# Narrow products of the mixing layers in three one-pass matmuls behind the first tile, FOX's log-sigmoid in ACT's second slot, values turned in the middle of a tile

## The reference

```python
for i in range(DEPTH):                       # first block, DEPTH = 4
    y = rmsnorm(h, norm_mix[i])
    mix = mixer(y, w_in[i], ...)             # FOX, GLA, GDN, FOX
    h = h + mix
    h = h + swiglu(rmsnorm(h, norm_ffn[i]), w_gate_up[i], w_down[i])
# FOX: y @ w_in = q, k, v, gate (1024 columns each) and f (16 columns)
#      q, k get a norm over each head; the scores get the running sum of log_sigmoid(f + b_f)
# GLA: y @ w_in = q, k (512 each), v, gate (1024 each) and a_lr (16 columns)
#      alpha = log_sigmoid(a_lr @ w_alpha2 + b_alpha) / 16
# GDN: y @ w_in = q, k, v, gate (1024 each), a (8 columns) and beta (8 columns)
#      g = -exp(a_log) * softplus(a + dt_bias), beta = sigmoid(beta)
```

## Time and profile before

| | |
|---|---|
| median of three runs | 2555.58 us |
| profiled execution, its span | 2551.63 us, 2549.8 us |
| TensorE matmul (PE) | 2338.9 us busy, 92% |
| TensorE weight load (PEld) | 2195.9 us, 86% |
| VectorE (DVE) | 1566.3 us, 61% |
| ScalarE (ACT) | 1215.1 us, 48% |
| GpSimd (POOL) | 621.2 us, 24% |
| DMA | 342.94 MB, mean 134 GB/s |
| TensorE clock granted, mean | 0.962 of full speed |
| ACT table loads | 71, of 1.28 us |

### The profile page before, as it was taken

The page is one execution under the profiler, slowest core; times in us unless marked ns, Lnnn a source line. Parts: engine busy times, 40 slices in busy tenths (PEclk is TensorE's granted clock), DMA queues, the critical chain, the costliest instruction groups (busy, mean ns, idle before and its releaser), DMA issues. The chain is left out here.

```text
span 2549.8 us, 47516 instructions
## 1 busy us (share of the span) xinstructions
PE 2338.9 (92%) x19162; PEld 2195.9 (86%) x19162; DVE 1566.3 (61%) x2510; ACT 1215.1 (48%) x1859; POOL 621.2 (24%) x744
## 2 busy tenths in 40 slices
PE   4999999899999898799989899996898998889998
PEld 3888999798998687699977789995698998778998
DVE  4665654645654665465546656546667975656994
ACT  4455544444543642455345554443445554444653
POOL 3114211013211030032121132213174540053550
PEclk8889999999999999899999999998999999989999
DMA  4223545323555221155442245453243554233554
GB/s 160 84 83 133 180 154 189 123 83 122 176 162 169 100 68 51 51 168 179 155 144 84 90 136 173 160 189 121 83 163 120 189 165 166 67 119 130 189 171 136
DMA packets 52715, 342.94 MB, mean 134 GB/s; under 512 B 5888, under 2 KB 7104, under 8 KB 20160
## 3 DMA queue, kind: packets, MB, share of 16 engines
q1 hardware_dynamic: 51984, 336.26, 39.9%
q0 software_dynamic: 560, 4.26, 0.4%
HBM read 339.38 MB, written 1.05 MB: 134 GB/s over the span
## 5 line engine op out<-in xcount | busy, mean ns | idle before, releaser
L729 PE MATMUL ps<-arena_r,ring_hi 128*128 128x272 f32 (+1 forms) x6688 | 1605.5, 289 | 15.6 <-DVE arena L2107 7.4
L729 PEld LDWEIGHTS ps<-arena_r,ring_hi 128*128 128x128 f32 x6688 | 1178.2, 192 | 19.9 <-DVE arena L2107 7.8
L729 PE MATMUL ps<-y_r,ring_hi 128*128 128x272 f32 (+1 forms) x3424 | 1024.5, 299 | 22.7 <-POOL arena_r L2843 10.2
L1983 DVE TENSOR_TENSOR ring_lo<-ring,ring_hi 128x2048 fp32r<-128x2048 f32 (+1 forms) x348 | 737.8, 2121 | 411.8 <-ACT ring_hi L1461 411.0
L729 PE MATMUL ps<-y_r,ring_lo 128*128 128x272 f32 (+1 forms) x3424 | 989.1, 289 | 0.0
L729 PEld LDWEIGHTS ps<-y_r,ring_hi 128*128 128x128 f32 x3424 | 659.8, 193 | 59.1 <-issue 25.6
L1461 ACT ACTIVATE ring_hi<-ring 128x2048 fp32r<-128x2048 f32 (+1 forms) x348 | 607.5, 1747 | 121.9 <-DMA ring<-dn 49.9
L729 PEld LDWEIGHTS ps<-y_r,ring_lo 128*128 128x128 f32 x3424 | 661.7, 193 | 0.0
L729 PE MATMUL ps<-arena_r,ring_lo 128*128 128x272 f32 (+1 forms) x1632 | 469.2, 287 | 0.0
L729 PEld LDWEIGHTS ps<-arena_r,ring_lo 128*128 128x128 f32 x1632 | 311.3, 191 | 0.0
L1461 ACT ACTIVATE arena<-arena 128x272 f32<-128x272 f32 (+7 forms) x199 | 93.4, 472 | 409.5 <-DVE arena L2538 268.8
(11 more groups left out here) (229 smaller groups left out, 1725.8 us busy)
## 6 DMA issues: line engine op xcount, KB each, us to landing
ring<-gu SPq DMA_DIRECT2D x88, 1024.0 KB, 5.0
ring<-dn SPq DMA_DIRECT2D x64, 704.0 KB, 4.0
ring<-up SPq DMA_DIRECT2D x44, 1024.0 KB, 5.1
ring<-fox_in SPq DMA_DIRECT2D x32, 1024.0 KB, 5.1
ring<-sdn SPq DMA_DIRECT2D x32, 704.0 KB, 4.0
ring<-gdn_in SPq DMA_DIRECT2D x16, 1024.0 KB, 5.1
ring<-in SPq DMA_DIRECT2D x16, 1024.0 KB, 5.1
ring<-gla_in SPq DMA_DIRECT2D x12, 1024.0 KB, 5.1
```

The lines of the kernel that those rows point to most:

```text
L729: return nc.tensor.matmul(dst, w, mv, start=start, stop=stop)
L1983: V.tensor_tensor(ring_lo[:, slot, 0:w], ring[:, slot, 0:w], ring_hi[:, slot, 0:w].bitcast(F32), ALU.subtract).then_inc(lo_ready, 1)
```

## The change

1. Two new tiles: `sw_hi` (128 columns, one mixer's at a time) and `sw_lo` (the low part of all). ACT writes the high part (`narrow_high`), VectorE the low part (`narrow_low`): for the first FOX layer before the first root, for the other mixers at the start of the SwiGLU's down projection ahead of them.
2. The narrow products are 24 one-pass matmuls behind tile 0 and behind `norm_sum`, in bank 6. In GDN the 8 columns of beta follow as 24 more, to bank 5, and both go to partition 0. FOX's tile of its own is gone (`EXTRA`).
3. FOX: VectorE's logits follow its taking of tile 0. ACT's log-sigmoid stands in slot 1, behind the weight split of that slot and before the square of tile 1. The table for Ln is loaded so that it serves the next root too: one load less in each FOX layer.
4. FOX: a v tile is turned in the middle of the tile after next, k of the next pair, and not behind q of the next pair.

```diff
@@ TensorE
+            def one_pass(dst, at, m, k):
+
+                hi, lo = sw_hi[:, at % P:at % P + m], sw_lo[:, at:at + m]
+                shi, slo = y_parts(k)
+                mm(dst, hi, shi, k == 0, False)
+                mm(dst, hi, slo, False, False)
+                return mm(dst, lo, shi, False, k == KC - 1)
+
+            def narrow(dst, at, m, layer, stride):
+
+                pe.wait_ge(sw_low, layer)
                 for k in range(KC):
-                    y_chunk(k)
-                    for part, a in enumerate(a.bitcast(F32) for a in y_parts(k)):
-                        last = mm(acc(n.tile, T, m), w[:, columns(k):columns(k) + m], a, k == 0 and part == 0, k == KC - 1 and part == 1)
-                last.then_inc(acc_ready, 1)
-                n.tile += 1
-                norm_sum()
+                    last = one_pass(dst, at + k * stride, m, k)
+                return last
...
-                pe.wait_ge(evacuated, n.tile + 1)
-                narrow(sw, lambda k: j * P + k * FH, FH)
...
+                def middle(t):
+                    if t >= 2 and FOX_TILES[t - 2][0] == "v":
+                        values_to_tokens(FOX_TILES[t - 2][1])
+
                 def after(t):
+                    if t == 0:
+                        narrow(ps[0:FH, 6, 0:T], j * P, FH, 1 + 3 * j, FH).then_inc(narrow_ready, 1)
                     for u in in_slot(units, t):
                         scores(u)
                     if t:
                         part, c = FOX_TILES[t - 1]
                         if part in "qk":
                             statistic(part, c)
-                        if part == "v":
-                            values_to_tokens(c)
                     for u in in_slot(units, t - 1):
                         turn(u)
                     slot = in_slot(units, t - 2)
                     if slot:
                         values(slot)
 
-                blocks(nb, tpb, kc, y_parts, T, y_chunk, after, 2)
+                blocks(nb, tpb, kc, y_parts, T, y_chunk, after, 2, middle)
...
-                def ready(k):
-                    y_chunk(k)
-                    if k == 0:
-                        pe.wait_ge(tables_loaded, 32)
-                    for part, a in enumerate(a.bitcast(F32) for a in y_parts(k)):
-                        last = mm(ps[0:GR, 6, 0:T], sw[:, 2 * P + k * GR:2 * P + (k + 1) * GR], a, k == 0 and part == 0, k == KC - 1 and part == 1)
-                    if k == KC - 1:
-                        last.then_inc(lr_ready, 1)
...
+                        narrow(ps[0:GR, 6, 0:T], 2 * P, GR, 2, GR).then_inc(lr_ready, 1)
...
-                def ready(k):
-                    y_chunk(k)
-                    for part, a in enumerate(a.bitcast(F32) for a in y_parts(k)):
-                        first, final = k == 0 and part == 0, k == KC - 1 and part == 1
-                        at = 3 * P + k * 2 * NH
-                        mm(ps[0:NH, 6, 0:T], sw[:, at:at + NH], a, first, final)
-                        last = mm(ps[64:64 + NH, 6, 0:T], sw[:, at + NH:at + 2 * NH], a, first, final)
-                    if k == KC - 1:
-                        last.then_inc(ab_ready, 1)
 
...
+                        narrow(ps[0:NH, 6, 0:T], 3 * P, NH, 3, 2 * NH)
+                        narrow(ps[0:NH, 5, 0:T], 3 * P + NH, NH, 3, 2 * NH).then_inc(ab_ready, 1)
@@ ACT
+                def log_sigmoid():
+                    act.wait_ge(f_ready, n.logit + 1)
+                    a = f_rows[0:FH, 2, :]
+                    step(fn(a, f_rows[0:FH, 1, :], ACT.Abs))
+                    step(fn(a, a, ACT.Sigmoid))
+                    ln_exp()
+                    fn(a, a, ACT.Ln).then_inc(fl_ready, 1)
+                    n.logit += 1
...
                     before(t)
+                    if t == 1:
+                        log_sigmoid()
...
+            def narrow_high(s):
+                fn(sw_hi[:, :], sw[:, s * P:(s + 1) * P], ACT.Copy).then_inc(sw_high, 1)
@@ VectorE
+                def forget_logits():
+
+                    v.wait_ge(narrow_ready, j + 1)
+                    step(V.tensor_tensor(f_rows[0:FH, 0, :], ps[0:FH, 6, 0:T], rstd[0:FH, :], ALU.mult))
+                    V.tensor_scalar(f_rows[0:FH, 1, :], f_rows[0:FH, 0, :], pcol(f"fox_b{j}")[0:FH, :], None, ALU.add).then_inc(f_ready, 1)
...
                     evacuate(t, part, c)
+                    if t == 0:
+                        forget_logits()
...
-                    V.tensor_tensor(R(4), ps[64:64 + NH, 6, 0:T], rstd[64:64 + NH, :], ALU.mult)
+                    V.tensor_tensor(R(4), ps[0:NH, 5, 0:T], rstd[0:NH, :], ALU.mult)
...
+            def narrow_low(s, done):
+                v.wait_ge(sw_high, done)
+                cols = slice(s * P, (s + 1) * P)
+                V.tensor_tensor(sw_lo[:, cols], sw[:, cols], sw_hi[:, :].bitcast(F32), ALU.subtract).then_inc(sw_low, 1)
```

More of the change, by code:

```diff
@@ L293, in build @@
         sw = sb("sw", 8 * P)
+        sw_lo = rounded_twin(sw, "sw_lo", 8 * P)
+        sw_hi = ctx.enter_context(nc.sbuf_tensor("sw_hi", [P, P], F32R))
         sq = sb("sq", 2, T)
@@ L343, in build @@
         tables_loaded = sem("tables_loaded")
+        sw_high = sem("sw_high")
+        sw_low = sem("sw_low")
+        narrow_ready = sem("narrow_ready")
         acc_ready = sem("acc_ready")
@@ L656, in memory_units @@
             return units
-        EXTRA = {"fox_in0": 1, "fox_in1": 1}
         @block.sync
@@ L670, in _ @@
             for name, nb, tpb, kc in plan:
-                tile += EXTRA.get(name, 0)
                 width = tpb * kc * P
@@ L1058, in after @@
                         steps[name](h)
-                blocks(nb, tpb, kc, y_parts, T, ready, after, 2, middle)
+                blocks(nb, tpb, kc, y_parts, T, y_chunk, after, 2, middle)
                 statistic(GH - 1)
@@ L1278, in at_half, with after @@
                             acts[name](*which)
-                blocks(nb, tpb, kc, y_parts, T, ready, lambda t: at_half(2 * t + 1), 2, lambda t: at_half(2 * t))
+                def after(t):
+                    if t == 0:
+                        narrow(ps[0:NH, 6, 0:T], 3 * P, NH, 3, 2 * NH)
+                        narrow(ps[0:NH, 5, 0:T], 3 * P + NH, NH, 3, 2 * NH).then_inc(ab_ready, 1)
+                    at_half(2 * t + 1)
+                blocks(nb, tpb, kc, y_parts, T, y_chunk, after, 2, lambda t: at_half(2 * t))
                 for p in range(2 * len(GDN_TILES), GDN_END + 1):
@@ L1472, in split, with norm_x @@
                 fn(ring_hi[:, slot, 0:w], ring[:, slot, 0:w], ACT.Copy).then_inc(hi_ready, 1)
-            def norm_x(src, gain, width, base, before=None, last=False):
+            def norm_x(src, gain, width, base, before=None, last=False, first=False):
                 for c in range(KC):
@@ L1486, in norm_x @@
                     fn(dst, src[:, c, :], ACT.Copy, scale=pcol(gain, c)).then_inc(y_ready, 1)
+                if first:
+                    act.wait_ge(tables_loaded, 32)
+                    narrow_high(0)
                 ln_exp()
@@ L1540, in fox @@
                 units = fox_units()
-                n.tile += 1
-                act.wait_ge(f_ready, n.logit + 1)
-                softplus_tail(f_rows[0:FH, 1, :], f_rows[0:FH, 2, :]).then_inc(fl_ready, 1)
-                n.logit += 1
-                ln_exp()
+                def log_sigmoid():
[6 more added lines that the diff above has]
+                    n.logit += 1
                 def rstd_of(part, c):
@@ L1920, in hybrid @@
                     n.out += KC
+            def narrow_high(s):
+                fn(sw_hi[:, :], sw[:, s * P:(s + 1) * P], ACT.Copy).then_inc(sw_high, 1)
             act.wait_ge(inputs_loaded, 48)
-            norm_x(x, "norm_mix0", T, None, split)
+            norm_x(x, "norm_mix0", T, None, split, first=True)
             for name, nb, tpb, kc in plan:
                 before = hooks(split, n, tpb)
+                if name in NARROW:
+                    narrow_high(NARROW[name])
                 if name.startswith("fox_in"):
@@ L2063, in fox @@
                 new_rstd(T)
-                step(V.tensor_tensor(f_rows[0:FH, 0, :], take(0, T, FH), rstd[0:FH, :], ALU.mult))
-                v.sem_inc(evacuated, 1)
-                V.tensor_scalar(f_rows[0:FH, 1, :], f_rows[0:FH, 0, :], pcol(f"fox_b{j}")[0:FH, :], None, ALU.add).then_inc(f_ready, 1)
                 step(V.tensor_scalar(gain8[:, :], pcol(f"fox_q{j}"), -(FD ** -0.5), None, ALU.mult))
-                n.tile += 1
+                def forget_logits():
+                    v.wait_ge(narrow_ready, j + 1)
+                    step(V.tensor_tensor(f_rows[0:FH, 0, :], ps[0:FH, 6, 0:T], rstd[0:FH, :], ALU.mult))
+                    V.tensor_scalar(f_rows[0:FH, 1, :], f_rows[0:FH, 0, :], pcol(f"fox_b{j}")[0:FH, :], None, ALU.add).then_inc(f_ready, 1)
                 def head_norm(part, c):
@@ L2690, in _ @@
             split(0, 1)
+            narrow_low(0, 1)
             for name, nb, tpb, kc in plan:
```

(4 more changed lines are left out.)

3 lines of the change are left out of this document (1 added, 2 removed).

## The result

The changed kernel takes 2512.38 us (median of 4 runs, 2502.33 to 2517.23) where the kernel before takes 2555.63 us (4 runs). The ratio is 0.984, with a 95% interval of 0.9819 to 0.9861. Run again on another chip, it took 2509.43 us against 2555.78, ratio 0.9809 (0.978 to 0.9838). The forecast was 2519.0, with 2509 to 2535 as range. The direction and most steps held. The gain of 43 to 46 us is larger than the forecast's 36.6.

The account below looks back on a forecast made before the run. TensorE, busy 92% of the span, was taken as the bound. Gains of 35.8 us off the profiled 2551.6 gave 2515.8; 3.2 added for the median made 2519 us, range 2509 to 2535.

Parts of the forecast that it names:

- Second FOX layer, 7.4: Second FOX layer's start: earlier norm sum and root move the head norm and first scores earlier, 7.4 us gained.
- First FOX layer, 7.0: First FOX layer's start: same chain as the second, but narrow passes partly at 1.2 GHz, 7.0 us gained.
- GLA, 11.7: GLA's start: alpha products 8.2 us earlier, then no wait and no low clock behind it, 11.7 us gained.
- GDN, 4.7: GDN's start: take of tile 1 earlier, although 48 narrow passes now run in sequence, 4.7 us gained.
- Values in mid-tile, 5.0: FOX layers: turning values half a tile later removes transpose waits but makes new ones; middle of 0 and 9.9 us.
- its 9.9: Most that turning values in mid-tile could gain: three pairs per layer, 3 x 2.3 + 3 x 1.0 us.
- Sum: All five gains together: 7.4 + 7.0 + 11.7 + 4.7 + 5.0 = 35.8 us off the profiled execution.
- The first (values worth nothing): FOX layers: low clock follows TensorE to the new waits, so turned values gain nothing; 2524 us, chance 0.18.
- The second: Layer starts run at 1.2 GHz because TensorE's work is thinner; about 16 us less gain, 2535 us, chance 0.08.
- The third: FOX starts: POOL's memset holds VectorE's weight split; 6.4 us less gain, 2525 us, chance 0.10.
- The fourth, the slower case: FOX layers: ACT copies turned values too late in each of 16 pairs, costing 38 us; 2562 us, chance 0.02.

Follow-up runs that it names:

- two runs that undo parts of them: Changed kernel with log-sigmoid and logits first again, 2520.09 us; changed kernel with the norm's sum behind the narrow products, 2517.43 us.

## Why the forecast was right, and where it was off

- **Second FOX layer, 7.4.** Right: head norm 7.8 us earlier, first scores 6.8. The wait at the k statistic, put at 4.8, was 3.2. The statistic of the q tile was put 11.2 us earlier and came 9.7, because part of the narrow passes ran at 1.2 GHz; it didn't matter, since the chain went through ACT and VectorE, as the forecast has it.
- **First FOX layer, 7.0.** Right: the head norm came at 42.64, worked out at 43.2, and the k statistic waited 4.44.
- **GLA, 11.7.** Right. The alpha products came 8.2 us earlier (466.39 to 448.17, less 10.03), the take of tile 2 11.3, forecast 11.8. The layer gave 14.6 and 13.0 in the two traces, of which the clock (0.94 to 0.97) is a part. No run took GLA's part out alone.
- **GDN, 4.7.** Right in size. The take of tile 1 came 4.4 us earlier (about 833.9 to 804.42, less 25.10); experiments gave 7.3 alone and 4.2 by layer. That the new products don't overlap held as well: joining them gave 3.0, the time of the 24 matmuls that go.
- **Values in mid-tile, 5.0.** This is the term that was mis-sized: 12.5 to 13.9 us when taken out (uncertainty 7) and 19.8 alone (13 to 24). The forecast took each wait of 2 us to be replaced by a new one of 2.1. The waits did come (six of 2.1), but they took the place not only of the transposes' long waits but of the eight short ones there and of shorter ones at the same statistics, so that the sum fell by 9.7 us against the changed kernel without this edit. I had called the other waits on line 902 worth nothing; they were part of it. The forecast halved its 9.9 because the low clock might follow the new waits: it did in one trace of the changed kernel and not in the other. By length times clock the edit is worth 8.4 us there and 4.3 in the kernel before, so the forecast's upper end, 9.9, was the better value; how much of what the medians show above that is clock, and how much noise, stays open.
- **Sum.** The excess of 7 to 10 us over the forecast's 36.6 is about what this one term was short by. The other four agree with theirs within what can be measured, but only GDN's was measured by itself. Those of the FOX starts and of GLA rest on the order of time and on two runs that undo parts of them.
- **Rivals.** The first (values worth nothing) fell by both experiments. The second came in part, at one of the four starts in each execution: 3.4 us at 1.2 GHz at the second FOX layer's start in the first trace, where 15 narrow passes follow each other every 0.227 us instead of 0.125, and as much at the first FOX layer's start in the second trace. GLA's and GDN's starts ran at 2.4 GHz in both, so its 16 us didn't come. (Its price for GDN was too high anyway: at 0.227 us, 48 passes lose 4.9 us and a tile 2.4.) The third fell by one row: VectorE's weight split at 1286.25 took its usual 2.29 us within POOL's memset (1285.99 to 1289.72). This agrees with the Trainium skill ("SBUF — State Buffer", Who interferes with whom), by which an instruction with two SBUF inputs contends only with a GpSimd instruction that reads. The last TENSOR_SCALAR of the logits, at 1289.26, took 0.61 us and ended only 0.15 us behind that memset, where the same instruction took 0.35 us in the second trace's first FOX layer, begun behind the memset. The fourth, the slower case, did not show: TensorE's waits for ACT's copies and exponentials are 15.9 us, longest 2.8, and were 15.6, longest 2.6: far from 38 us more.

## What to carry to other kernels

Where an early result (here the norm's sum) holds three engines, put it ahead of work that nobody waits for yet, and put long ACT work (table loads) behind the copies that feed the bottleneck. When a moved instruction trades one wait for another, add up all waits behind the same producer, short ones too, before and after; the long one alone misleads. And compare layers by length times granted clock before believing a difference of a few us from one trace. That product isn't the whole truth either: with the log-sigmoid in slot 2 it was 5.5 and 3.7 us higher in the two FOX layers than in the changed kernel, though both layers were shorter, since TensorE's waits now passed at the full clock and so counted in full.

## What the runs showed that was not expected

- The time at 1.2 GHz differs between two executions of one kernel by 10 us in one layer (first FOX, clock 0.94 and 0.96), and the medians of the kernel before lay between 2550.41 and 2555.78 on different chips. So 0.2% was too fine a bound for what one measurement tells: the 95% intervals here are 0.2 to 0.3% to each side.
- A kernel with more TensorE work (plain float32) had the higher clock in all four layers and lost 15 us (uncertainty 8) where its trace, at one clock, counts 25 to 27.
- Taking a wait of 4.44 us down to 0.93 moved the layer's scores by little, but from 40 to 60 us the clock was then 1.00 where it had been 0.84:

```profile
40.00:60.00 20.00, 13.36 (x99) 12.38 (x98) 12.06 (x23) 11.06 (x19) 1.21 (x2) 1.00 0.33 107
```

```profile
40.00:60.00 20.00, 12.88 (x77) 12.16 (x76) 12.57 (x24) 10.18 (x19) 1.59 (x3) 0.84 0.28 102
```

The first row is of the kernel with the log-sigmoid in slot 2, the second of the changed kernel's second execution. This isn't one execution's chance: in this stretch the two other kernels with the log-sigmoid in slot 2 had 0.95 and 1.00, and the six traces with it in slot 1 and one-pass narrow products 0.78 to 0.84. So the low clock there goes with the long wait ahead of it, and an edit that takes out a wait also changes the clock behind it.
